# The first weight tiles of each layer placed ahead of the decay projection and the norm's sum

## What is computed

```
h = rmsnorm(x, norm_mix)
z = h @ w_in                      # q, k, v; GLA q, k, v, gate; decay rank 16; two merge gates
oa = differential attention(q, k, v)           # 8 heads
g = log_sigmoid(ag @ w_ga2 + b_ga) / 16        # ag: 16 columns of z; 4 GLA heads of 128
og, S = gated linear attention(qg, kg, vg, g)  # 4 heads, in chunks of 64
x = x + (sigmoid(ga) * (oa @ w_pa) + sigmoid(gb) * (og @ w_pb)) @ w_o
h = rmsnorm(x, norm_ffn);  x = x + (silu(h @ w_f1) * (h @ w_f3)) @ w_f2
h = rmsnorm(x, norm_ple);  x = x + sigmoid(h @ w_ple_gate) * (pe @ w_ple)
```

## Time and profile before

| | |
|---|---|
| median of 3 runs | 1508.14 us (1506.59 to 1509.23) |
| profiled execution: its time, its span | 1513.19 us, 1511.4 us |
| TensorE busy, weight loads busy | 1420.7 us (94%), 1358.0 us (90%) |
| VectorE, ScalarE, GpSimd busy | 889.7 us (59%), 620.7 us (41%), 249.5 us (17%) |
| mean granted TensorE clock | 0.976 of full |
| HBM | 181.45 MB read, 8.65 MB written, 126 GB/s |
| chain that ended last | PE 65%, DVE 13%, DMA 8%, POOL 5%, issue 4%, ACT 4% |

### The profile page before, as it was taken

The page is one execution under the profiler, slowest core; times in us unless marked ns, Lnnn a source line. Parts: engine busy times, 40 slices in busy tenths (PEclk is TensorE's granted clock), DMA queues, the critical chain, the costliest instruction groups (busy, mean ns, idle before and its releaser), DMA issues.

```text
span 1511.4 us, 24369 instructions
## 1 busy us (share of the span) xinstructions
PE 1420.7 (94%) x9942; PEld 1358.0 (90%) x9942; DVE 889.7 (59%) x1423; ACT 620.7 (41%) x1040; POOL 249.5 (17%) x289
## 2 busy tenths in 40 slices
PE   5999998999999999999979999989989999999996
PEld 2989897888899999999969999878889999999995
DVE  3665666466556565545557566565756665564554
ACT  3445343444644333333344534334456343333332
POOL 1303021030005000022431030301200220000233
PEclk9999998999999999999989999999999999999998
DMA  6555589654344544544535756986443444544442
GB/s 157 109 110 128 111 100 107 104 133 99 115 140 140 166 141 142 168 133 159 141 62 104 129 131 93 110 97 130 103 128 114 152 153 140 166 150 140 147 154 70
DMA packets 195211, 191.69 MB, mean 127 GB/s; under 512 B 9078, under 2 KB 192188, under 8 KB 195100
## 3 DMA queue, kind: packets, MB, share of 16 engines
q1 hardware_dynamic: 189904, 181.62, 52.3%
q0 software_dynamic: 2688, 7.35, 1.3%
q10 hardware_dynamic: 2508, 1.16, 0.3%
HBM read 181.45 MB, written 8.65 MB: 126 GB/s over the span
## 4 chain that ended last, share of the span: by engine, by line
PE 65%; DVE 13%; DMA 8%; POOL 5%; issue 4%; ACT 4%; SPq 0%; DVEq 0%; POOLq 0%; ACTq 0%
PE big L1157 19%; PE big L1158 19%; PE big L1159 19%; DMA w_raw<-in_w_in 8%; DVE w_lo L822 3%; DVE sqt L1000 2%; POOL E L513 2%; POOL rot L520 1%; POOL E L514 1%; PE X L1428 1%; DVE a_msk L995 1%; PE X L1198 1%; ACT w_hi L545 1%; DVE E L980 1%; DVE E L979 1%
## 5 line engine op out<-in xcount | busy, mean ns | idle before, releaser
L1157 PE MATMUL big<-x_hi,w_hi 128*128 128x320 f32 x1984 | 633.3, 319 | 13.1 <-DVE z L900 7.2
L1158 PE MATMUL big<-x_lo,w_hi 128*128 128x320 f32 x1984 | 618.7, 312 | 0.0
L1159 PE MATMUL big<-x_hi,w_lo 128*128 128x320 f32 x1984 | 618.6, 312 | 0.0
L822 DVE TENSOR_TENSOR w_lo<-w_raw,w_hi 128x1024 fp32r<-128x1024 f32 (+1 forms) x330 | 415.8, 1263 | 159.4 <-ACT w_hi L545 157.8
L545 ACT CAST w_hi<-w_raw 128x1024 fp32r<-128x1024 f32 x328 | 330.1, 1035 | 203.7 <-DMA w_raw<-in_w_in 108.7
L1157 PEld LDWEIGHTS big<-x_hi,w_hi 128*128 128x128 f32 x1984 | 378.0, 191 | 24.2 <-issue 10.7
L1158 PEld LDWEIGHTS big<-x_lo,w_hi 128*128 128x128 f32 x1984 | 378.1, 191 | 2.1
L1159 PEld LDWEIGHTS big<-x_hi,w_lo 128*128 128x128 f32 x1984 | 377.7, 190 | 0.0
L477 POOL TENSOR_TENSOR sqt<-xT 128x320 f32<-128x320 f32 x48 | 52.7, 1098 | 622.7 <-DVE xT L1106 421.4
L1157 PE MATMUL big<-h_hi,w_hi 128*128 128x320 f32 x352 | 108.6, 309 | 0.0
L1158 PE MATMUL big<-h_lo,w_hi 128*128 128x320 f32 x352 | 108.4, 308 | 0.0
(11 more groups left out here) (226 smaller groups left out, 1803.5 us busy)
## 6 DMA issues: line engine op xcount, KB each, us to landing
w_raw<-in_w_in SPq DMA_DIRECT2D x130, 512.0 KB, 8.5
w_raw<-in_w_f SPq DMA_DIRECT2D x120, 512.0 KB, 4.5
w_raw<-in_w_pb SPq DMA_DIRECT2D x16, 512.0 KB, 4.5
w_raw<-in_w_pa SPq DMA_DIRECT2D x16, 512.0 KB, 4.4
w_raw<-in_w_o SPq DMA_DIRECT2D x16, 512.0 KB, 4.0
w_raw<-in_w_ple_gate SPq DMA_DIRECT2D x16, 512.0 KB, 4.7
w_raw<-in_w_f SPq DMA_DIRECT2D x16, 384.0 KB, 3.5
k_raw<-in_cache_k SPq DMA_DIRECT2D x8, 256.0 KB, 10.2
```

The source lines that it names most:

```text
L822: tt(w_lo[:, t % 4, 0:nk, :], w_raw[:, (t // 2) % 2, 0:nk, (t % 2) * P:(t % 2 + 1) * P], w_hi[:, t % 4, 0:nk, :].bitcast(F32), ALU.subtrac ...
L1157: mm(out, wh, xh[:, k0 + k, :], start=start and k == 0, stop=False)
L1158: mm(out, wh, xl[:, k0 + k, :], start=False, stop=False)
L1159: last = mm(out, wl, xh[:, k0 + k, :], start=False, stop=stop and k == nk - 1)
```

## The change

- TensorE: tile 0 of the mix stage comes first; the rank projection and the norm's sum follow it, tile 1 next, then the four heads, then tile 2. The wait for the pads moves to behind tile 5, with one for `zg`.
- ScalarE and VectorE: each layer casts and splits its own tiles 0 and 1, one ahead of and one behind the chunks of x. The two tiles cast behind the last gate tile are gone, and with them the two behind the whole of layer 1 and SyncE's load for them. In layer 0 the sum for the norm is made behind the split of tile 1, and the second table load of ScalarE is gone.
- The load of the constant tables and of layer 1's `w_ag` on ScalarE's queue is issued behind the cast of tile 1.
- The decay's bias, abs, exp and log are made for head 0 at t = 1, for the other three at t = 2 (bias) and t = 9 (the rest).
- `cur` is gone: each layer reads its parameters in `parT` and `c5` directly.

```diff
@@ scalar
-        for t in range(2):
-            act.wait_ge(raw_in[0], 32)
-            nc.scalar.copy(w_hi[:, t, :, :], w_raw[:, 0, :, t * P:(t + 1) * P]).then_inc(hi_ready, 1)
-            if t == 0:
+        act.wait_ge(consts_in, 16)
+        act.wait_ge(par_ready, 1)
+
+        for l in range(0, DEPTH):
+            if l:
+                tables(LN_EXP)
+            first, first8 = base(l, 0, MIX_N, 0)
+            hi(first, first8, 0, KC)
+
+            act.wait_ge(tile_done, first + CREDIT_TILE)
+            for m in range(KC):
+                act.wait_ge(x_ready, l * 24 + m + 1)
+                norm_chunk(l, 0, m, R_MIX)
+            hi(first, first8, 1, KC)
+            if l == 0:
                 act.dma_start(cst[:, K_COS:NCONST], A["consts"][:, K_COS:NCONST]).then_inc(tables_in, 16)
                 act.dma_start(w_ag[:, KC:, :], w_in[:, KC:, C_AG:C_AG + RANK]).then_inc(ag_in[1], 16)
-        act.wait_ge(consts_in, 16)
-
-        for l in range(0, DEPTH):
-            tables(LN_EXP)
-            act.wait_ge(cur_ready, l + 1)
-
-            act.wait_ge(x_ready, l * 24 + KC)
-            for m in range(KC):
-                norm_chunk(l, 0, m, U_MIX)
             norm_rstd(l, 0)
...
                 for t in range(MIX_N):
                     hi(tb, tb8, t + 2, KC)
+                    if j == 0 and t == 1:
+                        decay_log(0, 1, 0)
+                    if j == 0 and t == 9:
+                        decay_log(1, GH, 1)
@@ vector
+            if l:
+                w_agg_scaled(l)
+            lo(first, 0, KC)
             for m in range(KC):
-                lo_chunk(l, 0, m, U_MIX)
+                lo_chunk(l, 0, m, R_MIX)
+            if l == 0:
+                w_agg_scaled(l)
+            lo(first, 1, KC)
+            if l == 0:
+                sx = Steps(dve, dve_sum, 0, 3)
+                dve.wait_ge(xsum_ready, 6)
...
+                dve.wait_ge(tables_in, 16)
             dve.wait_ge(pads_ready, l * 5 + 5)
             dve.wait_ge(ag_done, l + 1)
             dve.wait_ge(rstd_ready, l * 3 + 1)
             tt(agT[:, :], X[1][0:RANK, 0:T], rstd[0:RANK, :], ALU.mult).then_inc(agT_ready, 1)
...
+                        if j == 0:
+                            decay_args(0, 1, 0)
+                        wait_plain(dve, consts_in, lg_ready, l * 2 + (1 if j == 0 else 2))
                         st.put(stt(E[:, NL, :], zg[:, j, :], 0.0, gab[:, j + (2 * KC - GH), :], ALU.min, ALU.subtract))
...
                     if t == 2:
                         out_tile(z[:, 0, :], t)
+                        if j == 0:
+                            decay_args(1, GH, 1)
@@ tensor
                 for t in range(MIX_N):
                     pe.wait_ge(result_read, rb + (t - 1 + CREDIT_RES))
                     tile(tb, t, x_hi, x_lo, chunk_wait=(xlo_ready, xc) if t == 0 else None)
+                    if j == 0 and t == 0:
+                        decay_rank()
+                    if j == 0 and t == 1:
+                        decay_heads()
+                    if j == 0 and t == 5:
+                        pe.wait_ge(zg_ready, l * 2 + 2)
+                        pe.wait_ge(pads_ready, l * 5 + 5)
@@ sync
-        sp.wait_ge(lo_ready, DEPTH * TILES + CREDIT_TILE - 2)
-        for r in range(0, KC, KC // 2):
-            sp.dma_start(w_raw[:, 0, r:r + KC // 2, :], w_in[:, r:r + KC // 2, 0:UW]).then_inc(raw_in[0], 16)
```

More of the change, by code:

```diff
@@ L573, in norm_chunk @@
         def norm_chunk(l, s, m, col):
-            nc.scalar.activation(x_hi[:, m, :], xT[:, m, :], ACT.Copy, scale=cur[:, col + m:col + m + 1]).then_inc(xhi_ready, 1)
+            nc.scalar.activation(x_hi[:, m, :], xT[:, m, :], ACT.Copy, scale=parT[:, col + l * KC + m:col + l * KC + m + 1]).then_inc(xhi_ready, 1)
         def norm_rstd(l, s):
@@ L788, in _ @@
                 for t in range(PLE_N):
-                    last = j == PLE_IT - 1
-                    if not (last and t >= 2):
+                    if j < PLE_IT - 1 or t < 2:
                         hi(tb, tb8, t + 2, KC)
@@ L827, in lo_chunk, with w_agg_scaled @@
             dve.wait_ge(xhi_ready, l * 24 + (8 * s + m + 1))
-            stt(x_lo[:, m, :], xT[:, m, :], cur[:, col + m:col + m + 1], x_hi[:, m, :].bitcast(F32),
+            stt(x_lo[:, m, :], xT[:, m, :], parT[:, col + l * KC + m:col + l * KC + m + 1], x_hi[:, m, :].bitcast(F32),
                 ALU.mult, ALU.subtract).then_inc(xlo_ready, 1)
-        st = Steps(dve, dve_pro, 0, 9)
+        def w_agg_scaled(l):
+            tt(w_agg[:, :, :], w_ag[:, l * KC:(l + 1) * KC, :], bc(parT[:, R_MIX + l * KC:R_MIX + (l + 1) * KC, None], [P, KC, RANK]),
+               ALU.mult).then_inc(agg_ready, 1)
+        st = Steps(dve, dve_pro, 0, 5)
         dve.wait_ge(consts_in, 16)
@@ L850, in _ @@
                 dve.wait_ge(par_trans, 1)
[L851 to L857, removed]
+                tt(parT[:, :], X[4][:, 0:NPAR], cst[:, K_GS:K_GS + NPAR], ALU.mult).then_inc(par_ready, 1)
@@ L858, in _ @@
+        dve.wait_ge(par_ready, 1)
         st.wait()
         st.close()
-        for t in range(2):
-            lo(0, t, KC)
         for l in range(0, DEPTH):
[L865 to L869, removed]
+            first = l * TILES
@@ new lines, in _ @@
+            if l == 0:
+                sx = Steps(dve, dve_sum, 0, 3)
+                dve.wait_ge(xsum_ready, 6)
+                sx.put(tt(x_tot[:, :], x_sum[:, :, 0], x_sum[:, :, 1], ALU.add))
+                sx.wait()
+                for t in range(2):
+                    sx.put(nc.vector.tensor_scalar(ssq[:, t * P:(t + 1) * P], ident, x_tot[:, t:t + 1], None, ALU.mult))
+                nc.vector.tensor_scalar(ssq[:, TP:T], ident[:, 0:TS], x_tot[:, 2:3], None, ALU.mult).then_inc(ssq_ready, 1)
+                sx.close()
+                dve.wait_ge(tables_in, 16)
@@ L878, in _, with decay_args @@
             tt(agT[:, :], X[1][0:RANK, 0:T], rstd[0:RANK, :], ALU.mult).then_inc(agT_ready, 1)
[L879 to L883, removed]
+            def decay_args(h0, h1, n):
+                dve.wait_ge(g_done, l * 2 + n + 1)
+                for h in range(h0, h1):
+                    ins = nc.vector.tensor_scalar(zg[:, h, :], X[2 + h][:, 0:T], parT[:, R_BG + GH * l + h:R_BG + GH * l + h + 1], None, ALU.add)
+                ins.then_inc(zg_ready, 1)
             for j in range(0, MIX_IT):
@@ L1128, in _ @@
                     tt(x, x, gs[:, :], ALU.add).then_inc(x_ready, 1)
-                    if last and t == PLE_N - 1:
-                        lo(tb, t + 1, KC)
-                        lo(tb, t + 2, KC)
         dve.wait_ge(rstd_ready, 3 * DEPTH + 1)
@@ L1192, in _, with decay_rank, decay_heads @@
         for l in range(0, DEPTH):
[L1194 to L1205 removed]
+            def decay_rank():
+                pe.wait_ge(x_ready, l * 24 + 8)
+                pe.wait_ge(agg_ready, l + 1)
+                for k in range(KC):
+                    last = mm(X[1][0:RANK, 0:T], w_agg[:, k, :], xT[:, k, :], start=k == 0, stop=k == KC - 1)
+                last.then_inc(ag_done, 1)
+                norm_sums(l * 3 + 1)
+            def decay_heads():
+                pe.wait_ge(ga2_in, l * 16 + 16)
+                pe.wait_ge(agT_ready, l + 1)
+                for h in range(GH):
+                    last = mm(X[2 + h][:, 0:T], ga2[:, h * GDK:(h + 1) * GDK], agT[:, :], start=True, stop=True)
+                    if h in (0, GH - 1):
+                        last.then_inc(g_done, 1)
             for j in range(0, MIX_IT):
```

63 lines of the change are left out of this document (22 added, 41 removed).

## The result

The changed kernel takes 1494.81 us (median of 4 runs, 1492.37 to 1497.06), the kernel before 1507.37 us on the same chip (4 runs, 1505.62 to 1509.23). The ratio is 0.9912, with a 95% interval of 0.9893 to 0.9931: 12.6 us by the medians, 13.3 by the ratio, against 15.6 forecast. The profiled execution has a span of 1493.8 us and took 1495.64 us; its span is 17.6 us shorter than that of before.

The account below looks back on a forecast made before the run. The prediction took TensorE, busy 94% of the span, as the bound, with a second chain through the decay to tile 6. Terms 6.9 + 6.4 + 2.3 = 15.6 us gave a median of 1492.5 us, range 1488 to 1501.5.

Parts of the forecast that it names:

- The length of tile 0: Layer 0: tile 0 runs 5.8 us cold, its last two matmuls warm, 6.1 us in all, ending at 26.5.
- the rank projection costs 0.27 us a matmul: Rank projection behind tile 0: its 16 matmuls run warm, 4.3 us in all, where layer 0 took 7.3 before.
- the lower price of the short logarithm: Head 0's decay on ScalarE: three operations on a quarter of the elements take 0.5 us each, 1.5 together.
- the chain and not the queue: Layer 0: the decay chain to tile 6 sets the gain at 6.9 us; TensorE's own queue would give 7.2.
- starts at 760.1, 3.1 us after the last x: Layer 1: VectorE splits tile 0 until 759.5, first x_lo at 760.0, TensorE starts tile 0 at 760.1.
- I take the middle: Layer 1: tile 0 ends at 765.8, between 765.1 with the clock rising after 3.5 us and 766.5 all cold.
- (a): Rival, both layers: clock low again for the rank projection, 0.53 us per matmul; gain 7 us, 1501 us; chance 0.15.
- (b): Rival, slower: clock stays low through tiles 0 to 5 with narrow matmuls between; about 1536 us; chance 0.04.
- (c): Rival, no effect: a weight transfer or semaphore holds tile 0 until its old time; nothing's chance 0.03.
- (d): Rival, more gain: later cold stretches, 1.6 to 2.9 us each, vanish or appear; over 20 us; chance 0.03.
- The term for the clock: End: TensorE's norm sum may run at 0.75 instead of 1.44 us because it comes earlier, 0.6 us more gain.

Follow-up runs that it names:

- the logarithm in one piece: Changed kernel with the decay's arguments and logarithms of all four heads made ahead of the first scan: 1503.37 us, ratio 0.9959.
- the old order: Changed kernel with rank projection and heads in front of tile 0 again, w_agg first on VectorE, no wait for the pads: 1496.42 us, ratio 0.9933.
- the rank projection first: Changed kernel with rank projection and norm's sum ahead of tile 0, heads behind tile 1, no wait for the pads: 1482.99 us, ratio 0.9838.
- the last kernel: Projection-first kernel with layer 1's w_agg scaled in layer 0's last gate tile, seven projection chunks not awaiting the last x, layer 0's norm total earlier: 1480.26 us.
- the gap kept busy: Changed kernel plus nine float32 matmuls with unused results in front of tile 0 of layer 1: 1489.70 us, ratio 0.9889.
- the changed kernel's repeat: Changed kernel run again with no edit, for the spread: 1491.77 us, ratio 0.9895 to the kernel before.
- the end alone: Kernel before, with only the load, casts and splits of weights behind the last tile of layer 1 removed: 1504.05 us, ratio 0.9981.
- the parameters in place: Kernel before, with only cur and its seven copies per layer gone: 1507.80 us, ratio 1.0006.

## Why the prediction was right, step by step

| | forecast | measured |
|---|---|---|
| tile 0 of layer 0 starts | 20.4 | 20.44 |
| it ends | 26.5 | 26.4 |
| norm's sum done (T) | 31.6 | 31.65 |
| tile 2 starts | 37.3 | 37.44 |
| b out | 40.7 | 40.72 |
| tile 6, idle before it | 54.2, about 1.5 | 54.22, 1.23 |
| layer 1, after LX: tile 0 | 3.1 | 3.5 |
| T | 13.9 | 15.0 |
| tile 2 | 19.6 | 20.8 |
| b out | 23.0 | 24.1 |
| layer 1's gain | 6.4 | 5.4 |
| end | 2.3 | 1.8 |

**Layer 0: 6.9 us forecast, 6.9 measured.** That the two agree to a tenth, and T and tile 6 to less, is in part luck. The length of tile 0 was taken from one stretch of 5.8 us at the low clock; the same instructions took 5.99, 5.83, 5.51 and 5.15 us in four executions whose code up to there is the same, and tile 6 came at 54.22, 54.81 and 53.55 us in the three of them that have the logarithm split. The terms themselves held. That the rank projection costs 0.27 us a matmul behind tile 0 held (4.48 us for 16), and so did the lower price of the short logarithm: 1.5 us for three operations. That the chain and not the queue is the bound shows in one distance: from the start of b to tile 6 it is 13.81 us before (47.32 to 61.13), 13.83 after, 13.81 with the logarithm in one piece, 13.81 in layer 1 with the old order and 13.81 there with the rank projection first. In every trace it is 13.8 to 13.9 where TensorE waits ahead of tile 6. Where it does not wait, the distance is 13.29 (layer 1 of the last kernel), 13.75 and 13.85 (the gap kept busy) and 14.57 us (layer 0 with the rank projection first): there the queue has a say.

**Layer 1: the mechanism right, two sizes off.** The step "starts at 760.1, 3.1 us after the last x" was 0.4 short, mostly since the split of tile 0 took 1.54 us and not 1.2 (it ran from 751.42 to 752.96 us, beside GpSimd's add of 751.02 to 751.88). The step "I take the middle" of a tile half and wholly at the low clock was 0.6 short: all but the last few matmuls ran at 0.27 us apiece, the tile took 6.3 us. From T to b it is 9.1 us in both layers, as the prediction had it. The rivals' question, whether one cold tile leaves the clock low for the projection (a), is answered by the rows: L1205 took 4.48 us in both layers. (b) did not occur, and (c) fell with the first line of the timeline. The later cold stretch of (d) is absent in both profiles of the changed kernel and present, at tile 2 of layer 0, in three of the other kernels.

**End: 1.7 us came, 0.6 did not.** Square and add fell to 0.72 and 0.86 us, as forecast. The term for the clock did not come: the norm's sum again took 1.44 us, at a granted clock of 0.50, although it came 1.7 us sooner after TensorE's last work. The rows of the prediction left less room for it than it says: 0.57 granted from 1497 to 1498 us means a fall at about 1497.1 and not 1497.4. Behind the same 3.93 us of idle time the sum took 0.81 us in the changed kernel's repeat, 0.95 in the kernel with the end alone, and between 0.81 and 1.44 in the others. Yet the end gets no shorter by it. The repeat, TensorE at its end, and then the transposes of the first profile:

```profile
1475.66 0.81 PE L1177 MATMUL X<-ssq,cst 128*128 128x320 f32 x2 [3.93 <-POOL ssq L472]
1478.18 5.38 PE L1465 MATMUL X<-cst,xT 128*128 128x128 f32 x24 [1.71 <-DVE xT L1142]
```
```profile
1483.50 4.26 PE L1465 MATMUL X<-cst,xT 128*128 128x128 f32 x24 [1.71 <-DVE xT L1142]
```

What the warm sum gained (0.63 us), the transposes lost at a granted 0.50 (1.12 us), and the end took 15.6 us against 15.3. So the step that failed here is the term of 0.6 us: it counted the clock at the sum and not at what follows.

**The sum.** 14.1 us by the spans against 15.6; 12.6 by the medians, 13.3 by the ratio, 15.8 (0.9895) in the second session. All lie inside the range of 1488.0 to 1501.5. What the profile's spans and the medians disagree by, 1 to 4 us, is the middle of the kernel: from tile 6 to LX the runs gave 688.7 to 695.9 us, and from tile 6 of layer 1 to the last x 690.8 to 695.2, with no order by edit. Of the first stretch the rows show where it varies (above), of neither what sets it off.

**The parts, by the runs alone:** the end 1.4 to 1.8 us; the parameters in place 0; the split of the logarithm 4.1 and 4.7 us in the two layers; the order 4.85 and 0.5, together with the place of zg that goes with it. Tile 0 ahead of the projection, the part that names the change, is worth less than nothing: putting the projection first again, without the wait for the pads, saved 2.0 and 5.1 us. In layer 0 the split and the order make 8.95 us together where the gain is 6.9: they overlap, because with either of them taken back the scan is late, whatever the other does.

## What to carry to other kernels

Where the bounding engine stands idle at a stage's start, ask first which of its queued work needs least of the others, and put that there: the projection that needs only x filled the 5.6 us that the changed kernel still left open, and in its last form was worth another 10.4 us ahead of the two tiles 6, beside the 12.3 us that the change gained there. A reordering on the busy engine pays only as far as the second chain (here norm's sum, decay, scan, GpSimd, tile 6) moves along, so follow that chain to the next point where the two meet, and shorten it in the same edit. After an idle gap, price the first tile wholly at the low clock (behind 5.57 us of idle time 17 to 21 of its 24 matmuls ran so).

## What was not expected of the hardware

At layer 0's start the record of the granted clock does not show the low level. TensorE's matmuls of tile 0 stand 0.267 us apart there, the pace that elsewhere goes with a granted 0.50, but the record says 1.00 (after, from 20 to 25 us):

```profile
20.00:25.00 5.00, 4.56 (x17) 1.00 0.67 195
```

So near the start of the program the pace of the matmuls tells the clock, and the record doesn't.

The same instructions at the same place can run at either level from one execution to the next, with TensorE busy all the time before. Tile 2 of layer 0, behind the heads, took 3.6 us in both profiles of the changed kernel and 5.15 us in the run with the gap kept busy, whose code of layer 0 is the same. TensorE from 36.8 to 42 us, first the changed kernel, then that run:

```profile
36.80:42.00 5.20, 5.20 (x34) 1.00 0.83 131
```
```profile
36.80:42.00 5.20, 5.20 (x26) 0.67 0.96 153
```

The same difference lies between the last two kernels: from 36 to 40 us the one with the rank projection first had a granted clock of 0.64 and the one with the projection earlier still 1.00. The second got through seven matmuls more, 1.0 us by 0.145 apiece. That made up for its later norm's sum (26.86 us against 26.2), and tile 6 came at 52.12 and 52.23 us. The Trainium skill (TensorE: Matmul & The Clock Gate, "The HAM clock gate (the "warmup" mystery)") says that where the rise falls varies by half a microsecond from run to run. Tile 0 of layer 0 agrees with that: 5.15 to 5.99 us in four executions.
